# Attention of one inference step: the second half of each result added before the next row maximum, the sample unit placed fourth in odd heads, and the first output weights and roundings written into the last attention steps

## The reference, cut to what matters

```
def fox_attend(q, c_q, pos_q, k, v, c_k, pos_k):
    s = jnp.einsum('bqhd,bkhd->bhqk', q, k).astype(jnp.float32) * (HEAD_DIM_B ** -0.5)
    bias = jnp.transpose(c_q, (0, 2, 1))[:, :, :, None] - jnp.transpose(c_k, (0, 2, 1))[:, :, None, :]
    mask = pos_k[None, :] <= pos_q[:, None]
    s = jnp.where(mask[None, None], s + bias, -jnp.inf)
    p = jax.nn.softmax(s, axis=-1)
    return jnp.einsum('bhqk,bkhd->bqhd', p.astype(v.dtype), v)
...
            mix_p = jnp.concatenate([conv_out, att.reshape(b, -1, ATT_B_CH)], axis=-1) @ w_out_even[i]
...
        xp = layer_norm(DEEPNORM_ALPHA * xp + mix_p, ln_mix_g[layer], ln_mix_b[layer])
```

## Time and profile before

| what | value |
|---|---|
| median of 3 runs | 2755.68 us (2751.33 to 2757.24) |
| the profiled execution, its own time | 2756.72 us |
| its span in the trace | 2755.1 us |
| PE matmul busy, whole span | 2581.8 us, 94% |
| first row maximum of attention, last one | 327.54 us, 601.22 us |
| first matmul of the output projection | 630.57 us |

### The profile page before, as it was taken

How to read it: one execution, slowest core, us unless ns; L and a number is a source line. 1 busy time by engine, 2 the same in 40 slices (tenths; PEclk the granted TensorE clock), 3 DMA queues, 4 the chain that set the end, 5 groups by cost and what they waited for, 6 DMA issues and landing times.

```text
span 2755.1 us, 38472 instructions
## 1 busy us (share of the span) xinstructions
PE 2581.8 (94%) x15545; PEld 2471.4 (90%) x15545; DVE 1357.0 (49%) x2034; ACT 711.6 (26%) x1218; POOL 427.2 (16%) x423
## 2 busy tenths in 40 slices
PE   7999588877899999999999999999999999999996
PEld 7999455557799999999999999988999999999995
DVE  4788755556753323333334644577433333333355
ACT  4110354444341111111111531225211111111114
POOL 3299233322200000000002200032000000000023
PEclk9999799998999999999999999999999999999998
DMA  7110412122011111111111221121111111111101
GB/s 230 50 31 0 137 57 70 54 86 93 25 52 47 40 38 47 47 46 47 44 34 47 60 91 46 38 101 38 47 47 47 41 37 46 46 39 40 45 16 65
DMA packets 169615, 152.55 MB, mean 55 GB/s; under 512 B 17057, under 2 KB 144337, under 8 KB 169432
## 3 DMA queue, kind: packets, MB, share of 16 engines
q1 hardware_dynamic: 161920, 133.92, 16.0%
q0 software_dynamic: 6208, 15.94, 1.8%
q10 hardware_dynamic: 1320, 0.24, 0.1%
HBM read 131.43 MB, written 18.93 MB: 55 GB/s over the span
## 4 chain that ended last, share of the span: by engine, by line
PE 87%; DVE 8%; issue 2%; ACT 2%; DMA 1%; SPq 0%; DVEq 0%; POOL 0%; ACTq 0%
PE PS L746 26%; PE PS L747 26%; PE PS L748 26%; PE PS L964 2%; DVE ST L1738 2%; PE PS L902 1%; DVE AL L1560 1%; PE PS L754 1%; PE PS L906 1%; PE PS L955 1%; DVE SPR L1666 1%; PE PS L919 1%; DVE RSD L1849 1%; PE PS L942 0%; PE PS L760 0%
## 5 line engine op out<-in xcount | busy, mean ns | idle before, releaser
L746 PE MATMUL PS<-AH,WHI 128*128 128x368 f32 x3360 | 1122.4, 334 | 43.6 <-DVE Y L1912 14.1
L747 PE MATMUL PS<-AL,WHI 128*128 128x368 f32 x3360 | 1114.8, 332 | 0.0
L748 PE MATMUL PS<-AH,WLO 128*128 128x368 f32 x3360 | 1111.3, 331 | 0.0
L746 PEld LDWEIGHTS PS<-AH,WHI 128*128 128x128 f32 x3360 | 635.3, 189 | 54.5 <-DVE Y L1912 18.2
L747 PEld LDWEIGHTS PS<-AL,WHI 128*128 128x128 f32 x3360 | 634.4, 189 | 2.8 <-issue 0.6
L748 PEld LDWEIGHTS PS<-AH,WLO 128*128 128x128 f32 x3360 | 634.7, 189 | 0.0
L1942 DVE TENSOR_TENSOR HF<-S,PS 128x368 f32<-128x368 f32 x132 | 70.9, 537 | 698.1 <-ACT S L1179 698.1
L746 PE MATMUL PS<-HH,WHI 128*128 128x368 f32 x1056 | 349.9, 331 | 3.2 <-DVE Y L1953 3.2
L747 PE MATMUL PS<-HL,WHI 128*128 128x368 f32 x1056 | 349.6, 331 | 0.0
L748 PE MATMUL PS<-HH,WLO 128*128 128x368 f32 x1056 | 349.3, 331 | 0.0
L1953 DVE TENSOR_TENSOR Y<-Y,PS 128x368 f32<-128x368 f32 x480 | 251.6, 536 | 154.9 <-PE PS L748 154.9
(11 more groups left out here) (267 smaller groups left out, 2250.9 us busy)
## 6 DMA issues: line engine op xcount, KB each, us to landing
RAW<-in_w_ffn_gate SPq DMA_DIRECT2D x44, 512.0 KB, 3.8
RAW<-in_w_ffn_up SPq DMA_DIRECT2D x44, 512.0 KB, 5.0
RAW<-in_w_ffn_down SPq DMA_DIRECT2D x44, 512.0 KB, 3.5
RAW<-in_w_in_even SPq DMA_DIRECT2D x20, 512.0 KB, 4.9
Y<-x_spill SPq DMA_DIRECT2D x16, 552.0 KB, 6.0
KR<-in_cache_k SPq DMA_DIRECT2D x32, 256.0 KB, 3.1
RAW<-in_w_in_odd SPq DMA_DIRECT2D x16, 512.0 KB, 4.5
x_spill<-Y POOLq DMA_DIRECT2D x3, 1472.0 KB, 6.5
```

What stands on the lines that cost most here:

```text
L746: pe.matmul(out, wh, xh, start=first, stop=False)
L747: pe.matmul(out, wh, xl, start=False, stop=False)
L748: return pe.matmul(out, wl, xh, start=False, stop=last)
```

## The change

It has these parts:

1. On DVE, `gathered` of unit n-6 stands before `peak` of unit n.
2. `HEADS` puts the sample unit fourth (r = 3) in odd heads, where it was seventh (r = 6). Its values product falls at r = 8 of the same head, where it was at r = 1 of the next; its transposes back are at r = 1 of the next head, where they were at r = 4. `queries` and `new_keys` move forward too.
3. `key_turn`: an even head h turns its own keys at r = 1 to 4 as before, and the first two blocks for h+1 at r = 7 and 8; an odd head turns the last two at r = 0 and 1. The order of SP's page loads follows.
4. At the seam: SP loads output weight pieces 0 and 1 as soon as the last sample values product is done; ACT and DVE round them within steps NU+1 to NU+3; half of the first roundings of the result (`mix_high(2)`, `mix_low(2)`) go into steps NU+3 and NU+4; the second `inverse_conv` comes after them.

```diff
@@ -69,8 +69,14 @@
 XB, TB = 6, 4
 F_BANK = (7, 0, 2)
-PAR8 = (1, 1, 0, 0, 1, 1, 0, 0)
-HEADS = tuple((0, 1, 2, 3, 4, 5) + ((None,) if h % 2 else ()) + ((6, 8, 7), (6, 7, 8))[PAR8[h]] for h in range(NH))
+HEADS = ((0, 1, 2, 3, 4, 5, 6, 7, 8),
+         (0, 1, 2, None, 3, 4, 5, 6, 7, 8),
+         (0, 1, 2, 3, 4, 5, 6, 8, 7),
+         (0, 1, 2, None, 3, 4, 5, 6, 8, 7),
+         (0, 1, 2, 3, 4, 5, 6, 7, 8),
+         (0, 1, 2, None, 3, 4, 5, 6, 7, 8),
+         (0, 1, 2, 3, 4, 5, 6, 8, 7),
+         (0, 1, 2, None, 3, 4, 5, 6, 8, 7))
 NU = sum(map(len, HEADS))
 LAG_T, LAG_V = 3, 5
 SAMPLE = None
@@ -351,7 +357,11 @@
         def key_turn(n):
             h, r = place(n)
-            return (h, r - 1) if h < NH and 1 <= r < 5 else None
+            if h == NH:
+                return None
+            if h % 2 == 0:
+                return (h, r - 1) if 1 <= r < 5 else (h + 1, r - 7) if 7 <= r < 9 else None
+            return (h, r + 2) if r < 2 else None
         UNITS, NB_KEYS, NB_UNIT, HALVES = [], {}, {}, {}
         for u in range(NU):
@@ -372,7 +382,7 @@
         SMP = [u for u, _, i, _, _ in UNITS if i is SAMPLE]
         WIDE = [u for u, _, i, _, _ in UNITS if i == 8]
         BACK = {u + LAG_V + 3: p for p, u in enumerate(SMP)}
-        assert all(place(n)[1] == 4 or n >= NU for n in BACK)
+        assert all(place(n)[1] == 1 or n >= NU for n in BACK)
         def norm_step(n, h0, r0):
@@ -476,11 +486,14 @@
             values(1)
             value_pages(0)
             for h in range(NH - 1):
-                if h and h % 2 == 0:
-                    value_pages(h // 2)
-                key_pages(h + 1)
-                if h:
+                if h % 2 == 0:
+                    key_pages(h + 1)
+                    if h:
+                        values(h + 1)
+                else:
+                    key_pages(h + 1)
                     values(h + 1)
+                    value_pages(h // 2 + 1)
             def residual(k):
@@ -508,10 +521,12 @@
             sp.wait_ge(qk_lo, 3 * NH)
             for k in range(KT):
                 if k == 6:
-                    sp.wait_ge(qk_done, 1 + SMP[-1])
+                    sp.wait_ge(pv_done, 2 + SMP[-1])
+                    for n in (0, 1):
+                        load(2 * ST_OUT0 + n, (2 * ST_OUT0 + n) % 4, out_rows(0, n))
                     sp.wait_ge(sb_done, NS // 2)
                     sp.wait_ge(att_evac, 1 + NU)
-                    for n in range(4):
+                    for n in (2, 3):
                         load(2 * ST_OUT0 + n, (2 * ST_OUT0 + n) % 4, out_rows(0, n))
                 residual(k)
             for n in range(4, 8):
@@ -635,7 +650,7 @@
                 gp.wait_ge(rc_ready, u + 1)
                 gp.nop(nofuse=True)
                 gp.tensor_scalar(PB[u % 4][0:m, 0:n], PB[u % 4][0:m, 0:n], ST4[0:m, 2, u:u + 1], 1.0, ALU.mult, ALU.mult).then_inc(pn_ready, 1)
-                if h % 2 and r == 3:
+                if h % 2 and r == 0:
                     new_keys(h // 2)
                 if h + 1 < NH and r in (4, 5):
                     gp.wait_ge(pn_ready, u + 1)
@@ -969,8 +984,7 @@
                 pe.wait_ge(att_evac, SMP[p] + 2)
                 pe.wait_ge(exp_done, WIDE[2 * p + 1] + 3)
-                if p < NC:
-                    pe.wait_ge(la_copy, p + 1)
+                pe.wait_ge(la_cen, 2 * min(p + 1, NC))
                 for c in range(HT):
                     mm = pe.transpose(PS[:, 2, P * c:P * c + P], RS[:, c * P:(c + 1) * P], IDN)
                 mm.then_inc(sb_done, 1)
@@ -978,7 +992,7 @@
             def conv_norm(c, s_in, s_res, h):
                 pe.wait_ge(exp_done, WIDE[h - 1] + 3)
-                pe.wait_ge(sb_evac, (h - 1) // 2)
+                pe.wait_ge(sb_evac, h // 2)
                 norm_product(ONES_H, YSA, s_in, s_res, c, 2)
             pe.wait_ge(lfr_in, 16 * NS * NPAGE)
@@ -1303,11 +1317,25 @@
                 head_high(0, part)
             act.wait_ge(cs_ready, 1)
             act.copy(CQ2[64:128, :], KBS[0:64, PAST:KS]).then_inc(cq_ready, 1)
+            def mix_high(q, src, cs=range(NC)):
+                for c in cs:
+                    act.copy(AH[:, 2 * q:2 * q + 2, chunk(c)], src[:, 2 * q % 4:2 * q % 4 + 2, chunk(c)]).then_inc(la_hi, 1)
+
             for n in range(NU + LAG_V + 1):
                 if n > LAG_V:
                     result(*UNITS[n - LAG_V - 1])
                 if n < NU:
                     expo(*UNITS[n])
+                if n in (NU + 1, NU + 2):
+                    act.wait_ge(pv_done, 2 + SMP[-1])
+                    split_centred(ST_OUT0, (n - NU - 1,))
+                if n == NU + 3:
+                    act.wait_ge(qk_done, NU)
+                    act.wait_ge(att_evac, 1 + FIRST[4])
+                    mix_high(2, QKV, (0, 1))
+                if n == NU + 4:
+                    act.wait_ge(sb_evac, NS // 2)
+                    mix_high(2, QKV, (2,))
                 if n == NU:
                     act.wait_ge(la_copy, NC)
                     act.activation(RSV[:], RSV[:], ACT.Sqrt, bias=EPS).then_inc(la_sd, 1)
@@ -1318,7 +1346,7 @@
                 h, r = place(n)
                 if n in BACK:
                     sample_result(BACK[n])
-                if h % 2 and r == 2 and n < NU:
+                if h % 2 and r == 1 and n < NU:
                     queries(h // 2)
                 c, q = norm_step(n, 1, 4), 0
                 if c is None:
@@ -1334,16 +1362,7 @@
                     act.copy(RSV[:, c, :], PS[:, 2, 0:C]).then_inc(la_copy, 1)
                 if h + 1 < NH and r in (3, 4):
                     head_high(h + 1, r - 3)
-            split_centred(ST_OUT0)
-
-            def mix_high(q, src):
-                for c in range(NC):
-                    act.copy(AH[:, 2 * q:2 * q + 2, chunk(c)], src[:, 2 * q % 4:2 * q % 4 + 2, chunk(c)]).then_inc(la_hi, 1)
-
-            act.wait_ge(qk_done, NU)
             act.wait_ge(att_evac, 1 + NU)
-            act.wait_ge(sb_evac, NS // 2)
-            mix_high(2, QKV)
             mix_high(3, QKV)
             split_centred(ST_OUT0 + 1)
             for k in range(HT):
@@ -1792,13 +1811,20 @@
                 dve.wait_ge(la_sd, 1)
                 dve.reciprocal(RSV[:, c, :], RSV[:, c, :]).then_inc(la_rs, 1)
+            def mix_low(q, cs=range(NC)):
+
+                for c in cs:
+                    src, qs = AEXT if q < 2 else QKV, slice(2 * q, 2 * q + 2)
+                    dve.wait_ge(la_hi, 3 * OUT_TILES[0].index(q) + c + 1)
+                    low(AL[:, qs, chunk(c)], src[:, 2 * q % 4:2 * q % 4 + 2, chunk(c)], AH[:, qs, chunk(c)]).then_inc(m_ready, 1)
+
             for n in range(NU + LAG_V + 1):
                 if 1 <= n < NU + 1:
                     inverse(*UNITS[n - 1])
+                if n > LAG_V:
+                    gathered(*UNITS[n - LAG_V - 1])
                 if n < NU:
                     peak(*UNITS[n])
-                if n > LAG_V:
-                    gathered(*UNITS[n - LAG_V - 1])
                 if LAG_T <= n < NU + LAG_T:
                     turned(*UNITS[n - LAG_T])
                 if n == 1:
@@ -1813,22 +1839,18 @@
                 h, r = place(n)
                 if h + 1 < NH and r in (5, 6, 7):
                     head_low(h + 1, r - 5)
-                if NU < n <= NU + 2:
-                    inverse_conv(n - NU - 1)
-            split_centred(ST_OUT0)
-
-
-            def mix_low(q):
-
-                for c in range(NC):
-                    src, qs = AEXT if q < 2 else QKV, slice(2 * q, 2 * q + 2)
-                    dve.wait_ge(la_hi, 3 * OUT_TILES[0].index(q) + c + 1)
-                    low(AL[:, qs, chunk(c)], src[:, 2 * q % 4:2 * q % 4 + 2, chunk(c)], AH[:, qs, chunk(c)]).then_inc(m_ready, 1)
+                if n == NU + 1:
+                    inverse_conv(0)
+                if n in (NU + 2, NU + 3):
+                    split_centred(ST_OUT0, (n - NU - 2,))
+                if n == NU + 4:
+                    mix_low(2, (0, 1))
+            mix_low(2, (2,))
+            inverse_conv(1)
+
             def mix_low_even(o):
-                if o == 0:
-                    mix_low(2)
                 if o == 1:
                     mix_low(3)
                 if o == 2:
```

## The result

The changed kernel took **2774.49 us** (median of 4 runs, 2773.60 to 2775.43), the kernel before beside it 2753.51 us (4 runs): ratio **1.0077**, 95% interval [1.0061, 1.0093], so slower. The forecast was 2764, range 2745 to 2778.

The account below looks back on a forecast made before the run. No engine was full; PE's waits in a loop of maximum, addition, values and scores bound attention. Attention +21, seam -13.6, its clock -2.7, plus 3 for attention's clock: 2755.7 + 8 = 2764 us, range 2745 to 2778.

Parts of the forecast that it names:

- The loop through ACT (part 1): Attention: next maximum waits behind the addition, which waits for ACT's PVT copy; the 35 us removed nearly all given back.
- removes 35 us of PE waits: Attention: with the addition ahead of the maximum, PE's 35.3 us of waits before products with values go away.
- nearly gone: Sign of a right forecast in attention: PE's waits for the addition nearly gone.
- The bank 6 wait (parts 2 and 3): Attention: key transposes wait for ACT's copy out of bank 6; waits up from 6.4 to some 15 to 20 us.
- The clock in attention: Attention: sparser PE work in steps of 4.5 to 5 us lowers its clock; 3 us added, bounds 0 and 9.
- The waits and the order in attention: Attention, heads 0 to 7: sum of step gains and losses without the added clock term, +21 us (20.6).
- Steps 7 and 8: Even heads: key transposes wait there; steps take 5.0 and 4.5 us, a loss of 1.5 and 1.8 each.
- Steps 0 and 1 of the four odd heads: Odd heads: moved key transposes cost 1.0 and 0.6 us, with small units and short exponentials.
- The seam: Last maximum to first projection matmul: 15.7 us against 29.35, or -13.6.
- the 2.7 of the clock: Projection start: without PE's idle stretch the full clock is kept, -2.7 us; nothing if the clock falls all the same.
- the clock falls in attention and at the seam: Rival: low clock stretches in each pair of heads and no clock gain at the seam, 2772 us or more; chance 0.15.
- The rival on the other side: Rival, seam wins: key transposes don't wait, or wait while PE would anyway; attention +4, total 2744 us; chance 0.2.

Follow-up runs that it names:

- e1: Kernel before with only DVE's addition moved ahead of the next maximum (part 1 alone): 2760.2 us, ratio 1.0023.
- e5: Changed kernel with key transposes on PE ahead of the unit's own blocks and their ACT copies ahead of the exponential: 2734.0 us, ratio 0.9929.
- e9: Changed kernel with redundant score matmuls added on PE ahead of the key transposes in steps 7 and 8 of even heads: 2765.8 us, ratio 1.0036.
- e4: Changed kernel without the seam part (part 4): 2784.6 us, ratio 1.0109.
- e2: Kernel before with the sample unit and key placement alone (parts 2 and 3): 2793.8 us, ratio 1.0148.
- e3: Changed kernel with DVE's addition put back behind the maximum (part 1 undone): 2779.2 us, ratio 1.0103.
- e12: Kernel before with key transposes ahead of the unit's blocks, their copies ahead of the exponential, and the addition ahead of the maximum: 2746.8 us, ratio 0.9973.
- e13: Changed kernel with key transposes ahead of the unit's blocks, their copies ahead of the exponential, but the addition behind the maximum: 2748.3 us, ratio 0.9979.

## Why the prediction was right, and which term was mis-sized

- **The loop through ACT (part 1)** was right in what it comes to: about nothing in attention by itself (-2.1 in e1), with 62.7 us of DVE's waits for ACT. That no maximum passes the waiting addition holds in every trace here. But "removes 35 us of PE waits" was not so: PE still waits 25.3 of 37.3 us in e1 and 15.2 of 35.3 in the changed kernel, where the sign was "nearly gone". What I missed is a gain that this part has only together with part 2: the sample values start a maximum earlier.
- **The bank 6 wait (parts 2 and 3)** was right and is shown by e5: the waits are 29.3 us (15 to 20 forecast), 21.7 of them in steps 7 and 8 of even heads, and turning one order round takes 40 us off. Freed of the clock in e9, steps 7 and 8 of head 2 take 5.18 and 4.58 us, and the forecast was 5.0 and 4.5.
- **The clock in attention** is the term that was mis-sized: "I add 3", bounds 0 and 9. Steps 7 and 8 of the four even heads take 50.0 us in the changed kernel; at e9's full-clock 5.18 and 4.58 they would take 39.0, so 11 us are clock by this estimate. Steps 0 and 1 of heads 3 and 7 take 6.8 us more than in e4, at 0.50 instead of 0.95 and more. That makes 17.8 us, twice my upper bound. I had read the sparse steps, but not that the 2.6 us of standing still come just in front of the step's whole PE work, which then runs at 1.2 GHz and is all on the path.
- **The waits and the order in attention** then come to 14.5 us (32.3 less 17.8), and I had 20.6. Steps 7 and 8 cost 10.1 at the full clock instead of 13.2, because I took head 2's 6.03 us as what all even heads had before, and the kernel before needs 7.96, 7.97 and 7.00 in heads 0, 4 and 6. Steps 0 and 1 of the four odd heads cost 4.3 without the low stretches instead of 6.4. So two errors of opposite sign met in attention. The 20.6 and the 17.8 together would have given some 2781 us, above the range; that it held is in part luck.
- By heads: odd heads +4.4, +7.4, +3.2 (4.3 each forecast), even ones +4.4, +1.8, +3.4 (1.3 each), head 0 +4.7 (3.8), head 7 +3.0 (0). Head 4 loses less only because the kernel before was itself slow there (35.0).
- **The seam:** 17.06 for 15.7. Of the 2.7 of the clock little came (by its own rows it was 7.4 less 4.5, or 2.9): 626 to 642 us has a granted clock of 1.00, then PE waits 2.28 us in the tail, and the first projection matmuls again come at 0.31 us from one to the next, 8 of them instead of 19. But the stretch from the first of them to the first squaring of `Y` is as long as before, 86.7 for 86.6. Length and clock together were put at -16.3; -12.3 came.
- Together: attention 8 us over the forecast +24, the seam 4 short of its -16.3, and 1.9 gained ahead of attention, which no term had, are the 10 us between 2764 and 2774.5.
- The rival "the clock falls in attention and at the seam", 2772 or more, was nearest, and had 0.15. The rival on the other side asked for key waits that cost nothing. They did cost in this order of PE's work; e5 shows that in another order they nearly don't, and that then 2734 is the result.

Open: what puts the clock's low stretches where they are. Steps 0 and 1 of head 3 take 10.3 us in one kernel and 6.9 in another with the same instructions there, at 0.50 and 0.97. Of the 14 us of attention between e2 and e4, 6.8 are again these two steps in heads 3 and 7 (20.7 us in e2, 13.9 in e4; 18.7 in e3 and 20.7 after); why the rest of the difference is missing between e3 and after was not found. Why the projection has 0.91 in e1 and 0.95 in the kernel before is open too.

## What to carry to other kernels

When work is moved into a step of an in-order engine, ask what shares its buffer there and where the copy that frees it stands on the other engine; here 40 us lie between the same transposes behind the unit's blocks and ahead of them. An idle stretch of TensorE right in front of the work that the loop waits for can be paid twice, once as the wait and once as matmuls at half the rate (3.4 and 2.9 us in a pair of steps of heads 2 and 6); where the order is free, let that work go before the wait. Read a step's cost before from every head that has it, not from one. A part that is worth nothing alone (the addition's place, e12) can be worth 14 us with others (e13), so test a part with the others in place as well as alone.

## What the runs showed of the hardware

- Redundant matmuls in a wait made a kernel faster: 2774.5 to 2765.8 us, with the transposes behind them at 0.66 instead of 1.06 us. The Trainium skill (TensorE: Matmul & The Clock Gate, HAM oscillation) says that matmuls after an idle gap start cold; step 7 of head 2 in the changed kernel agrees (2.55 us of idle, then a granted clock of 0.61 in the next 4.4), and e9's head 4 (12.16 for 12.38) shows that filling the gap isn't always enough.
- Behind the seam no edit of the orders in attention changes anything, yet from ACT's first squaring of `Y` to the end the profiles have between 2030.2 (e5) and 2037.9 us (before), and from the first projection matmul to that squaring between 86.5 (e9) and 93.1 us (e4): so much of a difference between two single profiles is no effect shown of an edit.
